# Second mixer's first queries: product in two column halves, rotation by two heads, turns and scores moved up

## What is computed

```python
def dsa_mixer(hn, positions, w_in, w_out):
    B, S, _ = hn.shape
    proj = hn @ w_in
    q, k, v, qi, ki, wi = jnp.split(proj, ODD_SPLITS, axis=-1)
    q = rope(q.reshape(B, S, ATT_HEADS, ATT_HEAD_DIM), positions)
    k = rope(k.reshape(B, S, ATT_KV_HEADS, ATT_HEAD_DIM), positions)
    v = v.reshape(B, S, ATT_KV_HEADS, ATT_HEAD_DIM)
    qi = rope(qi.reshape(B, S, IDX_HEADS, IDX_DIM), positions)
    ki = rope(ki.reshape(B, S, 1, IDX_DIM), positions)[:, :, 0]
    o = dsa_attention(q, k, v, qi, ki, wi)
    return o @ w_out
```

## Time and profile before

| | before |
|---|---|
| median of 3 runs | 1488.12 us (1487.93 to 1488.16) |
| profiled execution | 1489.13 us |
| its span | 1486.1 us |
| TensorE busy | 1472.2 us, 99% |
| VectorE, ScalarE, GpSimd busy | 867.3, 710.9 and 91.4 us |
| granted TensorE clock, mean | 0.999 |

### The profile page before, as it was taken

The page is one execution under the profiler, slowest core; times in us unless marked ns, Lnnn a source line. Parts: engine busy times, 40 slices in busy tenths (PEclk is TensorE's granted clock), DMA queues, the critical chain, the costliest instruction groups (busy, mean ns, idle before and its releaser), DMA issues.

```text
span 1486.1 us, 16921 instructions
## 1 busy us (share of the span) xinstructions
PE 1472.2 (99%) x7067; PEld 1227.9 (83%) x7067; DVE 867.3 (58%) x1007; ACT 710.9 (48%) x837; POOL 91.4 (6%) x115
## 2 busy tenths in 40 slices
PE   9999999999999999999999999999999999999999
PEld 6888888888888888888888888888888878888887
DVE  6464556665545555459764545655555887665543
ACT  6444355544434443345654443544435766454432
POOL 0000003000000000006200000000000800000000
PEclk9999999999999999999999999999999999999999
DMA  9655463455555655545455556565556543556552
GB/s 321 229 185 168 159 213 114 142 199 186 182 183 184 198 180 189 182 136 170 142 184 182 187 172 195 173 205 190 168 183 215 185 142 106 179 198 198 171 183 71
DMA packets 145105, 265.65 MB, mean 179 GB/s; under 512 B 7134, under 2 KB 27318, under 8 KB 144774
## 3 DMA queue, kind: packets, MB, share of 16 engines
q1 hardware_dynamic: 143174, 259.11, 53.2%
q0 software_dynamic: 1136, 4.35, 0.9%
q10 hardware_dynamic: 720, 1.11, 0.2%
HBM read 263.52 MB, written 1.05 MB: 178 GB/s over the span
## 4 chain that ended last, share of the span: by engine, by line
PE 93%; DVE 3%; POOL 2%; ACT 1%; DMA 1%; issue 0%; ACTq 0%; SPq 0%; DVEq 0%; POOLq 0%
PE ps L534 29%; PE ps L536 29%; PE ps L535 29%; PE ps L582 2%; PE ps L565 1%; POOL d_tmp L2097 1%; DVE wlo L1516 1%; DMA raw<-in_ffn_wi 1%; PE ps L743 1%; PE ps L647 1%; POOL d_q L2099 0%; PE ps L683 0%; PE ps L942 0%; PE ps L650 0%; PE ps L684 0%
## 5 line engine op out<-in xcount | busy, mean ns | idle before, releaser
L1516 DVE TENSOR_TENSOR wlo<-raw,whi 128x2048 fp32r<-128x2048 f32 (+3 forms) x268 | 566.9, 2119 | 419.8 <-ACT whi L1126 419.4
L1126 ACT CAST whi<-raw 128x2048 fp32r<-128x2048 f32 (+3 forms) x268 | 473.6, 1770 | 450.8 <-PE ps L536 446.4
L534 PE MATMUL ps<-whi,xt_hi 128*128 128x512 f32 (+3 forms) x1376 | 533.5, 388 | 1.3 <-DVE xt_lo L1530 0.7
L536 PE MATMUL ps<-whi,xt_lo 128*128 128x512 f32 (+3 forms) x1376 | 527.0, 383 | 0.0
L535 PE MATMUL ps<-wlo,xt_hi 128*128 128x512 f32 (+3 forms) x1376 | 526.8, 383 | 0.0
L534 PEld LDWEIGHTS ps<-whi,xt_hi 128*128 128x128 f32 x1376 | 258.6, 188 | 51.8 <-DVE xt_lo L1530 1.3
L536 PEld LDWEIGHTS ps<-whi,xt_lo 128*128 128x128 f32 x1376 | 258.5, 188 | 50.5
L535 PEld LDWEIGHTS ps<-wlo,xt_hi 128*128 128x128 f32 x1376 | 258.8, 188 | 47.7
L1152 ACT ACTIVATE junk<-X 128x512 f32<-128x512 f32 x40 | 25.4, 635 | 43.4 <-DVE X L1573 40.0
L534 PE MATMUL ps<-whi,yt_hi 128*128 128x512 f32 (+3 forms) x108 | 42.9, 397 | 2.1 <-DVE yt_lo L1528 1.2
L536 PE MATMUL ps<-whi,yt_lo 128*128 128x512 f32 (+3 forms) x108 | 41.7, 387 | 0.0
(11 more groups left out here) (387 smaller groups left out, 1601.0 us busy)
## 6 DMA issues: line engine op xcount, KB each, us to landing
raw<-in_ffn_wi SPq DMA_DIRECT2D x79, 1024.0 KB, 5.1
raw<-in_ffn_wo SPq DMA_DIRECT2D x40, 1024.0 KB, 5.1
raw<-in_ffn_w_gate SPq DMA_DIRECT2D x20, 1024.0 KB, 4.9
raw<-in_ffn_w_up SPq DMA_DIRECT2D x20, 1024.0 KB, 5.0
raw<-in_ffn_w_down SPq DMA_DIRECT2D x20, 1024.0 KB, 4.9
raw<-in_w_in SPq DMA_DIRECT2D x14, 1024.0 KB, 5.1
raw<-in_ffn_wi SPq DMA_DIRECT2D x16, 512.0 KB, 4.6
raw<-in_even_w_in SPq DMA_DIRECT2D x6, 1024.0 KB, 5.3
```

The lines of the kernel that those rows point to most:

```text
L534: e.matmul(o, h, hi_w, start=i == 0 and j == 0, stop=False)
L536: t = e.matmul(o, l, hi_w, start=False, stop=(end or (v == len(plan) - 2 and tt == 1)) and j == nk - 1)
L1126: e.copy(whi[0:n, v % SPLIT, c], raw[0:n, v % RAW, c]).then_inc(s_hi.mark(*[(v, j) for j in js]), 1)
L1516: e.tensor_tensor(wlo[0:n, v % SPLIT, c], raw[0:n, v % RAW, c], whi[0:n, v % SPLIT, c].bitcast(F32), ALU.subtract).then_inc(s_lo.mark(*[(v ...
```

## The change

The product of `dq0` is made in two halves of 256 columns, two heads each, each into a pair of PSUM banks of its own and from the same `whi` and `wlo` slots. ScalarE scales each half when it is done, and GpSimd rotates each half by itself. On TensorE `query_turn(0)` moves from behind `dq1` to the middle of its second block, and `head_scores(0)` ahead of all of `dv`. On ScalarE one cast moves behind the eviction of the index queries, one moves behind the first half's scaling, and the eviction of the turn comes ahead of the scaling of `dq1`. On VectorE the `unit()`s move later: one from ahead of the index sums to behind the first selection, one from ahead of the logits to between the logits of the two row blocks.

```diff
+                def half_steps(half, i, j0=0, j1=4):
+
+                    v = dq0.at[i]
+                    k0, nk, n = dq0.blocks[i]
+                    pair = take((dq0.name, half)) if (i, j0) == (0, 0) else Pair((dq0.name, half))
+                    for j in range(j0, j1):
+                        for tt in range(2):
+                            kt = k0 // 128 + j
+                            q.wait_ge(*s_dve[dq0.key, kt])
+                            q.wait_ge(*s_lo[v, j])
+                            c = j * 512 + 256 * half
+                            hi_w, lo_w = (w[0:n, v % SPLIT, c:c + 256] for w in (whi, wlo))
+                            h, l = (a[0:n, kt, 128 * tt:128 * tt + 128] for a in (XT.hi, XT.lo))
+                            o = pair.ap[:, tt, 0:256]
+                            e.matmul(o, h, hi_w, start=i == 0 and j == 0, stop=False)
+                            e.matmul(o, h, lo_w, start=False, stop=False)
+                            t = e.matmul(o, l, hi_w, start=False, stop=i == 1 and j == nk - 1)
+                            if j == nk - 1:
+                                names = [(v, tt)] if half else []
+                                if i == 1:
+                                    names.append(("dq0", half, tt))
+                                t.then_inc(s_mm.mark(*names), 1)
+
...
-                steps(dq0, 0, 0, 2)
+                half_steps(0, 0, 0, 2)
                 index_turn()
-                steps(dq0, 0, 2, 3)
+                half_steps(0, 0, 2)
                 index_scores()
-                steps(dq0, 0, 3)
-                steps(dq0, 1, 0, 2)
+                half_steps(0, 1)
+                give((dq0.name, 0), s_act["dq", "half", 0])
+                half_steps(1, 0)
                 key_turn()
-                steps(dq0, 1, 2)
-                give(dq0.name, s_act["dq", 0])
+                half_steps(1, 1)
+                give((dq0.name, 1), s_act["dq", 0])
                 steps(dq1, 0)
-                steps(dq1, 1)
+                steps(dq1, 1, 0, 2)
+                query_turn(0)
+                steps(dq1, 1, 2)
                 give(dq1.name, s_act["dq", 1])
-                query_turn(0)
-                steps(dv, 0, 0, 2)
                 head_scores(0)
-                steps(dv, 0, 2)
+                steps(dv, 0)
                 scored(dat, 0)
...
+                def queries(half):
+                    for tt in range(2):
+                        q.wait_ge(*s_mm["dq0", half, tt])
+                        t = e.mul(dQ[:, tt, 256 * half:256 * half + 256], Pair((dq0.name, half)).ap[:, tt, 0:256], RS[:, tt:tt + 1])
+                    t.then_inc(s_act.mark(("dq", "half", half), *([("dq", 0)] if half else [])), 1)
...
-                unit()
                 q.wait_ge(*s_turn["iq"])
                 e.copy(QIT[:, :, :], Pair("iq").flat[0:64, :].rearrange("p (h t) -> p h t", h=4)).then_inc(s_act.mark("qit"), 1)
+                unit()
...
+                queries(0)
                 unit()
                 q.wait_ge(*s_turn["dkt"])
                 e.copy(dKT[:, :, :], Pair("dkt").flat[:, 0:512].rearrange("p (g t) -> p g t", g=2)).then_inc(s_act.mark("dkt"), 1)
-                scaled(("dq", 0), lambda tt: dQ[:, tt, 0:512], dq0, RS)
+                queries(1)
...
+                query_turn(0)
                 scaled(("dq", 1), lambda tt: dQ[:, tt, 512:1024], dq1, RS)
-                query_turn(0)
...
                 select()
+                unit()
                 select()
...
-                unit()
-                logits(dat, 0, 0, bias)
+                logits(dat, 0, 0, bias, None, (1,))
+                unit()
+                logits(dat, 0, 0, bias, None, (0,))
...
-                q.wait_ge(*s_act["dq", 0])
-                for tt in range(2):
-                    rotate(dQ[:, tt, 0:512].rearrange("p (h b f) -> p h b f", h=4, b=2), 4, 0, 1, 64, room2, tt, ("dq", 0) if tt else ("dq", 0, 0))
+                for half in range(2):
+                    q.wait_ge(*s_act["dq", "half", half])
+                    for tt in range(2):
+                        rotate(dQ[:, tt, 256 * half:256 * half + 256].rearrange("p (h b f) -> p h b f", h=2, b=2), 2, 0, 1, 64, room2, tt,
+                               ("dq", 0) if (half, tt) == (1, 1) else ("dq", "half", half, tt))
```

More of the change, by code:

```diff
@@ L1727, in rotate, with logits @@
                 e.tensor_tensor(x, a, b, ALU.add).then_inc(s_dve.mark(name), 1)
-            def logits(at, g, i, over, before=None):
+            def logits(at, g, i, over, before=None, halves=(1, 0)):
                 name = at.name
-                for tt in (1, 0):
+                for tt in halves:
                     L, c = at.part(i, tt)
@@ L1879, in dsa @@
                     e.tensor_scalar(wi[:, tt, :], Iq[:, tt, 320:324], 1.0 / 16.0, None, ALU.mult).then_inc(s_dve.mark(), 1)
-                unit()
-                q.wait_ge(*s_turn["ik"])
-                e.tensor_copy(KIT[:, :], Pair("ik").flat[0:64, 0:256]).then_inc(s_dve.mark("kit"), 1)
                 q.wait_ge(*s_rows["all"])
@@ L1885, in dsa @@
                     e.tensor_scalar(held[tt][0], causal[:, tt, 0:128 * (tt + 1)], OUTSIDE, None, ALU.mult).then_inc(s_dve.mark(), 1)
+                q.wait_ge(*s_turn["ik"])
+                e.tensor_copy(KIT[:, :], Pair("ik").flat[0:64, 0:256]).then_inc(s_dve.mark("kit"), 1)
                 unit()
```

## The result

| | before | changed |
|---|---|---|
| median of 5 runs each, taken together | 1487.93 us (1486.55 to 1488.16) | 1493.43 us (1492.76 to 1493.96) |
| ratio | | 1.0035, 95% interval 1.0023 to 1.0047 |
| profiled execution, its span | 1489.13, 1486.1 us | 1493.43, 1491.4 us |

The change makes the kernel 5.5 us slower by these medians. 1492.6 was forecast with a range from 1490.5 to 1494.9, so the forecast was 0.8 low and the range holds the time.

A forecast was written before the change was run, and what follows sets the result against it. TensorE, busy 99% of the span, was taken as the bound. Waits of 7.9 - 4.1, matmuls 0.6 and small waits 0.1 made +4.5 us on the 1488.12 median: 1492.6 us, range 1490.5 to 1494.9.

The forecast's parts named there:

- Product in halves, +0.6 and small waits: TensorE, dq0's product: 96 matmuls of 256 columns for 48 of 512 cost +0.6 us, plus waits of 0.1 and 0.1.
- First rotation from 686.4 to 701.7: GpSimd, first queries: four half rotations take 10.3 us plus 5.0 for three VectorE subtractions, ending only 2.0 us earlier.
- TensorE at `query_turn(0)` at 699.7, a wait of 2.1: TensorE's first turn: reached at 699.7, it waits 2.1 us until 701.8 for GpSimd, with the second queries' product behind it.
- GpSimd idle 5.3 us, the second rotation from 707.0: GpSimd between query rotations: idle 5.3 us, as the second queries' product ends at 705.5; start at 707.0 instead of 703.87.
- Second rotation 12.8 us: GpSimd, second queries: 11.4 us as before, plus 1.2 and 0.3 for VectorE's normalising products, ending at 719.8.
- Wait of 5.8 at 719.8: TensorE at query_turn(1): arrives at 714.0, waits 5.8 us, begins the turn at 719.8 instead of 715.31, +4.5 us.
- The clock: the same 1.7 us: TensorE behind the second turn: a low-clock stretch again costs 1.7 us, as before, so no difference.
- clock stays up: Rival, TensorE's clock: both idles pass without a fall, +4.5 - 1.7 gives 1490.9; chance 0.10.
- first rotation in time: Rival, GpSimd: first rotation ends by 699.7, so the first turn costs nothing; +1.1 us, 1489.2; chance 0.07.
- GpSimd keeps the ports: Rival "Faster": GpSimd holds the memory ports throughout, so VectorE doesn't block its rotations; -3.5 us, 1484.6; chance 0.06.
- Slow half rotations: Rival, GpSimd's first rotation: 3.1 us a block, ending 2 us later and all else with it; +6.5, 1494.6; chance 0.11.
- The clock as a rival for the whole loss: Rival named with the experiments: the low-clock stretches that follow TensorE's waits cost the time; no size or chance given.

The follow-up runs named there:

- VectorE back: The changed kernel with VectorE's order of before, all four weight subtractions where they were: 1490.48 us, 1.0012 of the kernel before.
- turn back: The changed kernel with TensorE's order of before (query_turn(0) behind all of dq1) and ScalarE scaling dq1 ahead of the eviction: 1487.73 us, 0.9993 of the kernel before.
- halves alone: The kernel before with product, scaling and rotation in halves, without the moved turn, scores, eviction or VectorE's unit()s: 1490.51 us, 1.0011 of the kernel before.
- share: The kernel before with the second rotation's row block 1 on VectorE; with d_out's subtraction behind the normalising products ("subtraction late"): 1488.26 us, 1.0002.
- product alone: The kernel before with only dq0's matmuls and their scaling in halves, rotation still by four heads: 1488.73 us, 1.0003 of the kernel before.
- turn up alone: The kernel before with only the turn and the scores moved, on TensorE and ScalarE, no halves: 1497.71 us, 1.0056 of the kernel before.

## Why the prediction was right, by its steps

- **Product in halves, +0.6 and small waits.** Right. The waits were 0.15 and 0.35 us instead of 0.1 and 0.1. The second is one of the prediction's own signs of being wrong, a wait for `wlo` ahead of the second queries. It is small, and doesn't go "straight on the path" as was said: it comes off the wait at the first turn.
- **First rotation from 686.4 to 701.7.** Measured 686.31 to 701.84, with three subtractions on it as said. "VectorE back" confirms the price of a long one (2.66 us for an addition of 0.74), but there the short one cost GpSimd nothing: it met the addition of 698.16, which took 0.74, and VectorE was the one that waited (1.63 us instead of 1.22).
- **TensorE at `query_turn(0)` at 699.7, a wait of 2.1.** The size was off: it came at 700.7 and waited 1.31. A start 0.25 us later and waits of 0.15 and 0.35 where 0.2 was allowed make 0.55 us of it. The rest is what a stop takes beyond the wait that the profile names: the matmul ahead of it isn't overlapped, and lasts 0.28 us where a step is 0.12 (691.62 to 692.25 is 0.63 us, with 0.35 called a wait). That is 0.16 us at each of these two stops, and 0.07 more in the first matmul behind the second. As GpSimd's end sets the turn, the turn itself came at 702.0, as forecast (701.8).
- **GpSimd idle 5.3 us, the second rotation from 707.0: the step that decides.** Measured 5.35 and 707.19. But the prediction calls the idle itself a loss ("TensorE waits for GpSimd and then GpSimd for TensorE"), and "VectorE back" shows that it isn't: the idle is 5.51 us there, with no wait at the first turn. The loss is the late end of `dq1`'s product. Of the 3.1 us by which the rotation starts later in the stage than before, "turn back" takes away 2.4; the other 0.6 are there too when the turn is back, from the longer product and the stops ahead of the second queries. Nor is the moved turn by itself the cause: "VectorE back" against "halves alone" shows no cost in the medians. The step holds as the prediction worked it out, for a first rotation that ends behind TensorE's arrival.
- **Second rotation 12.8 us.** Measured 12.98. The added pieces are as named; the first subtraction (710.04) fell on the addition, 2.32 instead of 1.30.
- **Wait of 5.8 at 719.8.** Measured 5.87, at 720.32. TensorE's sum was +3.8 in waits, +0.6, +0.1; it is +3.0, +0.6, +0.5, and some 0.6 us that no wait holds: the stops at 677.14, 692.25 and 711.31 (`dv`'s `wlo`) take that much beyond their waits. The step of the stage is +4.8, where +4.5 was forecast. What TensorE loses ahead of a turn comes off its wait there, as GpSimd's end sets the turn; so the sum is near, though its pieces aren't.
- **The clock: the same 1.7 us.** Right in the sum, by half as luck: the low stretch doubled, and the idle took half of it.
- **The 0.8 us that the forecast was low** are this 0.3, the start 0.25 us later, and the 0.3 in the third mixer, for neither of which the prediction had a term. Neither is of the change: the start differs by execution, and the 0.3 is in all the other kernels too. That sum is for the spans, which differ by 5.3.

The rivals: *clock stays up* and *first rotation in time* did not come about, but the second is real: "VectorE back" is that case, and lay 1.8 us over its before where +1.1 was worked out (1489.2). The second rotation was 0.5 us longer than the 11.4 supposed, and the low clock, supposed as before, had 5.21 us of work in it instead of 3.41, which is 0.9 us. *GpSimd keeps the ports* is excluded by the 3.77 groups. *Slow half rotations* is excluded by the groups of 1.72 and 1.86.

The clock as a rival for the whole loss is excluded: it takes 1.7 us in the changed kernel and took 1.7 before. The twice as long stretch that the prediction named beside the slow half rotations did come, but half of it was idle time. But it is part of what separates the kernels of the experiments.

Still open is why the clock falls after one idle and not after another. Idles of 1.60 and 1.50 us ("turn back") and of 2.14 and 2.04 us ("share", subtraction late) brought no fall in the profiled executions, while 2.14 and 2.00 did before.

## What to carry to other kernels

When an early result is asked for earlier in an in-order queue, look at what stands behind the waiting instruction: if that work feeds the same helper engine, the wait delays the helper's next job, and the later wait can grow by more than the earlier one shrinks. Where the helper is done before the instruction is reached, the same move cost nothing that the medians show (1490.51 against 1490.48 us). A pause of the helper is not the loss; the date of its next input is. The price of one edit depended on the others (VectorE's moves changed the time by -2.8 us in one order of TensorE and by +2.9 in the other), so find the queue that ends last after each step, shorten that (here half a rotation on VectorE, placed where GpSimd is done), and only then move the turn up.

## What was not expected of the hardware

- The clock falls or stays up by execution in the same kernel. The eleven runs of "product alone" lie in two groups: four at 1487.22 to 1487.65 us with a mean granted clock of 1.000, seven at 1488.57 to 1489.77 with 0.999. The middles of the two groups are 1.7 us apart, what one low stretch of 3.41 us full of work costs. That it is such a stretch is an inference from the mean clock: the one profiled execution (1487.58) is of the fast group and has none. A single profile shows one of the two.
- The low stretches behind these waits lasted 3.41 or 6.83 us; what one costs is half of TensorE's busy time inside it: 1.7 us (changed kernel), 2.6 ("VectorE back"), 2.6 and 3.0 ("turn up alone").
- VectorE and GpSimd, each with four products of 128x256 float32, lengthened one another unequally: 1.43 to 3.64 us on VectorE, 2.93 to 3.38 on GpSimd. Against one long subtraction it is GpSimd that loses, 1.72 to 3.77. Against a short one it was either: an addition grew from 0.74 to 1.58 in the changed kernel (subtraction 1.35), and stayed at 0.74 in "VectorE back" (subtraction 1.63 instead of 1.22).
